# Seven-product weight units: two PSUM banks for the weight sums in place of three

## The reference, cut to what matters

```python
def swiglu(h, w_in, w_out):                      # first block, D_FF = 2816
    a, b = jnp.split(h @ w_in, 2, axis=-1)
    return (jax.nn.silu(a) * b) @ w_out
...
f = jnp.square(jax.nn.relu(h @ mlp_w1[i])) @ mlp_w2[i]     # second block, i = 0, 1; D_FF_2 = 4096
```

## Time and profile before

| what | value |
| --- | --- |
| median of 3 runs | 2633.7 us (2633.25 to 2634.71) |
| the profiled execution's own time | 2629.4 us |
| its span, first to last instruction | 2627.6 us |
| PE busy | 2569.7 us, 98% of the span |
| DVE, ACT, POOL busy | 53%, 45%, 41% |
| mean granted PE clock | 0.997 of full speed |
| HBM traffic | 102 GB/s over the span |

### The profile page before, as it was taken

The page is one execution under the profiler, slowest core; times in us unless marked ns, Lnnn a source line. Parts: engine busy times, 40 slices in busy tenths (PEclk is TensorE's granted clock), DMA queues, the critical chain, the costliest instruction groups (busy, mean ns, idle before and its releaser), DMA issues.

```text
span 2627.6 us, 40349 instructions
## 1 busy us (share of the span) xinstructions
PE 2569.7 (98%) x15940; PEld 2160.0 (82%) x15940; DVE 1388.7 (53%) x2479; ACT 1192.8 (45%) x2071; POOL 1076.0 (41%) x501
## 2 busy tenths in 40 slices
PE   8999999999999999999999999999999999999998
PEld 6887788888777777899977678899887778889997
DVE  4566543343533338353658857455445564744554
ACT  4454422222543345453543845445445774534543
POOL 2222343443323324464633634555542112555552
PEclk9999999999999999999999999999999999999999
DMA  8622244543222211232232022323331112232332
GB/s 325 239 97 96 96 161 151 198 160 114 92 73 73 73 65 58 83 118 94 96 100 96 18 73 93 100 87 99 112 105 61 45 49 73 87 103 86 104 103 82
DMA packets 49843, 271.62 MB, mean 103 GB/s; under 512 B 5583, under 2 KB 9319, under 8 KB 25608
## 3 DMA queue, kind: packets, MB, share of 16 engines
q1 hardware_dynamic: 45648, 265.71, 29.4%
q10 hardware_dynamic: 4024, 3.54, 0.6%
HBM read 267.09 MB, written 2.13 MB: 102 GB/s over the span
## 4 chain that ended last, share of the span: by engine, by line
PE 68%; issue 22%; POOL 5%; DVE 3%; ACT 1%; POOLq 0%; ACTq 0%; DVEq 0%
PE lin L879 14%; PE lin L881 13%; PE lin L880 13%; PE lin L1959 6%; PE lin L1960 6%; PE lin L1961 6%; POOL wlo L756 5%; PE lin L1431 2%; PE bank L1415 1%; PE bank L1449 1%; PE bank L1610 1%; PE bank L1028 0%; PE lin L1435 0%; PE bank L1602 0%; PE lin L1602 0%
## 5 line engine op out<-in xcount | busy, mean ns | idle before, releaser
L756 POOL TENSOR_TENSOR wlo<-raw,whi 128x1024 fp32r<-128x1024 f32 (+4 forms) x202 | 696.9, 3450 | 1309.7 <-ACT whi L2101 1309.7
L2101 ACT ACTIVATE whi<-raw 128x1024 fp32r<-128x1024 f32 (+4 forms) x202 | 295.4, 1462 | 601.1 <-PE lin L881 541.6
L879 PE MATMUL lin<-hhi,whi 128*128 128x512 f32 x1160 | 465.4, 401 | 7.4 <-issue 2.6
L881 PE MATMUL lin<-hhi,wlo 128*128 128x512 f32 x1160 | 453.3, 391 | 0.0
L880 PE MATMUL lin<-hlo,whi 128*128 128x512 f32 x1160 | 452.4, 390 | 0.0
L879 PE MATMUL lin<-ghi,whi 128*128 128x512 f32 x1136 | 445.8, 392 | 2.5 <-ACT m L2121 1.7
L881 PE MATMUL lin<-ghi,wlo 128*128 128x512 f32 x1136 | 442.3, 389 | 0.0
L880 PE MATMUL lin<-glo,whi 128*128 128x512 f32 x1136 | 442.2, 389 | 0.0
L777 POOL TENSOR_TENSOR wlo<-raw,whi 128x512 fp32r<-128x512 f32 x200 | 265.9, 1343 | 174.4 <-ACT whi L2433 172.2
L879 PEld LDWEIGHTS lin<-hhi,whi 128*128 128x128 f32 x1160 | 218.2, 188 | 68.6 <-issue 14.9
L881 PEld LDWEIGHTS lin<-hhi,wlo 128*128 128x128 f32 x1160 | 218.0, 188 | 47.1
(11 more groups left out here) (538 smaller groups left out, 4400.6 us busy)
## 6 DMA issues: line engine op xcount, KB each, us to landing
raw<-in_w SPq DMA_DIRECT2D x139, 1024.0 KB, 4.9
raw<-in_w SPq DMA_DIRECT2D x85, 512.0 KB, 3.6
adw_a<-in_ada SPq DMA_DIRECT2D x30, 1024.0 KB, 5.0
adw_b<-in_ada SPq DMA_DIRECT2D x18, 1024.0 KB, 5.5
raw<-in_w SPq DMA_DIRECT2D x12, 768.0 KB, 5.6
raw<-in_w SPq DMA_DIRECT2D x8, 640.0 KB, 3.9
raw<-in_w SPq DMA_DIRECT2D x8, 384.0 KB, 3.1
x<-in_x SPq DMA_DIRECT2D x1, 2048.0 KB, 9.8
```

The lines of the kernel that those rows point to most:

```text
L756: nc.gpsimd.tensor_tensor(wlo[:, slot, 0:size], raw[:, slot, 0:size], whi[:, slot, 0:size].bitcast(F32), ALU.subtract).then_inc(s.wlo_ok, 1)
L879: pe.matmul(dst, lh, rh, start=first, stop=False)
L881: return pe.matmul(dst, ll, rh, start=False, stop=last)
L2101: act.activation(whi[:, slot, 0:size], raw[:, slot, 0:size], ACT.Copy).then_inc(s.whi_ok, 1)
```

## The change

The third sum no longer has bank B7. It goes into B4, which sum 1 and low 1 used before it, and so can be made only after low 1 has read B4. The instruction moves from `seven_sums` into `block_low`, behind low 1, with a wait for sum 2 and for low 1. High 5 and low 5 read B4 in place of B7. In ACT's `mlp`, which prepares the first unit of the first run, high 2 and high 3 move from behind the sixth gate tile to behind the eighth. The waits in `block_high` stay as they are: high 2 still waits for the third sum.

```diff
@@ block_high (ACT)
-                       4: weight_block(u, 0, 1), 5: as_block(B7), 6: weight_block(u, 1, 1)}[k]
+                       4: weight_block(u, 0, 1), 5: as_block(B4), 6: weight_block(u, 1, 1)}[k]
@@ mlp (ACT)
-                    for j in {5: (0, 1, 2, 3), 7: (4, 5, 6)}.get(k, ()):
+                    for j in {5: (0, 1), 7: (2, 3, 4, 5, 6)}.get(k, ()):
                         block_high(st.u + 2, j)
@@ seven_sums (DVE)
                 v.tensor_tensor(as_block(B5), as_block(B4), weight_block(u, 0, 0), ALU.subtract).then_inc(s.sum_ok, 1)
-                v.wait_ge(s.sum_ok, HAD["sum_ok"] + 3 * g + 2)
-                v.tensor_tensor(as_block(B7), weight_block(u, 1, 0), as_block(B5), ALU.subtract).then_inc(s.sum_ok, 1)
@@ block_low (DVE)
-                v.tensor_tensor(block_of_four(wlo, b), as_block({1: B4, 2: B5, 5: B7}[k]), block_of_four(whi, b).bitcast(F32),
+                v.tensor_tensor(block_of_four(wlo, b), as_block({1: B4, 2: B5, 5: B4}[k]), block_of_four(whi, b).bitcast(F32),
                                 ALU.subtract).then_inc(s.blk_lo_v, 1)
+                if k == 1:
+                    v.wait_ge(s.sum_ok, HAD["sum_ok"] + 3 * g + 2)
+                    v.wait_ge(s.blk_lo_v, HAD["blk_lo_v"] + 3 * g + 1)
+                    v.tensor_tensor(as_block(B4), weight_block(u, 1, 0), as_block(B5), ALU.subtract).then_inc(s.sum_ok, 1)
```

## The result

The changed kernel takes **2679.89 us** (median of 4 runs, 2679.0 to 2681.97) against 2633.47 us (4 runs, 2632.56 to 2634.71): a ratio of 1.0181 [1.0169 to 1.0194], 46.4 us slower. The forecast was 2679 us. The profiled execution's span grew from 2627.6 to 2677.8 us; the granted clock is 0.997 of full speed in both.

What follows compares the result with a forecast made beforehand. PE, busy 98% of the span, was taken to bound the kernel. Terms 22.6 + 13.9 + 0.3 + 3.0 + 2.6 + 3 = 45.4, say 45 us, on a median of 2633.7 gave 2679 us, range 2662 to 2696.

Steps and rivals of the forecast that it cites:

- The chain: Third sum between low 1 and low 2 adds a second trip DVE, ACT, DVE; c22 comes 1.41 us later.
- Units inside a run: 1.16 us in each of 12 `ffn_short` units, 13.9 us; 1.41 us in each of 16 `mlp` units, 22.6 us.
- The slack of 0.32 us: In `ffn_short`, c22 would allow product 6 0.32 us before PE gets there; in `mlp` the slack is nil.
- the closed cycle: In `mlp`, product 6, results' work, sums, low 1, low 2, c22, product 6 form a loop, so each unit pays 1.41 us.
- The very first unit: First of the 50 units, where PE already waits on low 1, low 2 and c22: 3 us taken, upper bound 4.3.
- the upper bound's third term: In the very first unit, 1.44 us for twelve matmuls at half the clock, added to two chains of 1.41 us.
- First units of later runs: Product 6 comes late by 0.1 us in `ffn_short`, 0.43 in `mlp`; with stalls 0.3 us and 3.0 us in all.
- starts of `mlp`: First run of each `mlp`: two more high parts on ACT delay product 2 by 0.8 us; 1.3 us each, 2.6 together.
- signs named: PE waits for c22 about 40 us in some 36 places of 0.1 to 1.5 us; ACT waits for third sum 50 times.
- The clock did not fall at the stalls: Rival, 7%: PE's granted clock falls at each unit's stall, 52 us more in 36 units, 2731 us in all.
- Sum 1 did not get shorter by itself: Rival, 6%: on DVE sum 1 starts ahead of POOL's subtraction and takes about 0.70 us, not 1.80; time 2648 us.
- Low 1 did not move up: Rival, 5%: not slower, as low 1 on DVE starts 0.69 us earlier once sum 3 leaves; time stays at 2634 us.

Runs made afterwards that it cites:

- ACT's order alone: The kernel before with only ACT's order at the start of the first `mlp` run as in the change: 2633.79 us, 1.0006.
- the third experiment: The kernel before, three banks and third sum in its old place, but high 2 waits for low 1, ACT's `mlp` order as in the change: 2650.31 us, 1.0068.
- the best version: Changed kernel with third sum behind c22, POOL waiting for sum 1, DVE reordered in the very first unit and at `mlp` starts: 2627.56 us, 0.9982 against the kernel before.

## Why the prediction was right

**The chain** was right in kind, and a little short. Predicted: 1.41 us. Measured: the third sum starts 0.11 us after low 1 ends (1180.67 to 1180.78), not 0.04; all other steps are as predicted (0.70, then 0.09 from the sum's end at 1181.48 to high 2, 0.60, and 0.03 to low 2). C22 is 1.48 us later. The gap was taken from sums 1 and 2, where one semaphore is waited for; the third sum waits for two. The kernel before had rows nearer to the case: the second unit's sum 1, which waits for two semaphores, one of them given by low 5, starts 0.11 us after low 5 ends:

```profile
1051.23 0.68 DVE L3488 TENSOR_TENSOR wlo<-bank,whi 128x512 fp32r<-128x512 f32 x1
1052.02 0.70 DVE L3478 TENSOR_TENSOR bank<-raw 128x512 f32<-128x512 f32 x1
```

With this gap the predicted delay would have come out at 1.48 us. That the second semaphore is the reason was not tried.

**Units inside a run.** The slack of 0.32 us in `ffn_short` and of nil in `mlp` held, and so did the closed cycle: 11.31 and 11.64 us against 11.24 and 11.57 predicted, each 0.07 us more for the one gap. The terms become 12 x 1.23 = 14.8 us for 13.9, and 16 x 1.48 = 23.7 us for 22.6.

**The very first unit** was sized too small: its run grew by 6.3 us, and without two units of 1.23 us that leaves 3.8 us for it, inside the bounds of 1.4 and 4.3, but not the 3 taken. Its waits on PE, in the place of the earlier trace rows:

```profile
1045.40 0.39 PE L1959 MATMUL lin<-thi,whi 128*128 128x256 f32 x1 [1.30 <-DVE wlo L3486]
...
1051.35 0.44 PE L1959 MATMUL lin<-thi,whi 128*128 128x256 f32 x1 [4.26 <-DVE wlo L3486]
...
1061.39 0.36 PE L1959 MATMUL lin<-thi,whi 128*128 128x256 f32 x1 [2.53 <-DVE lin L3546]
```

The wait for low 2 went from 1.74 to 4.26 us, and that for c22 hardly changed, 2.42 and now 2.53 us. As predicted, high 2 holds up an activation on ACT (line 2249), and DVE stands idle for it ahead of low 2:

```profile
1047.88 0.69 DVE L3593 TENSOR_TENSOR sq<-tmp,lin 128x512 f32<-128x512 f32 x1 [1.73 <-ACT tmp L2249]
```

From product 0, low 2 came 2.4 us later by this, not one chain of 1.41 us, and c22 another 1.5 us later. Both delays together are the 3.9 us by which product 6 came later (18.9 us behind product 0, before 15.0), so the upper bound's third term, twelve matmuls at half the clock, did not come on top. The clock did fall behind both waits, where before it fell behind one, but behind low 2 PE's slower work fitted into the wait for c22. The third row is a stretch of the steady units:

```profile
1051.50:1055.00 3.50, 3.50 (x18) 3.50 (x19) 3.50 (x2) 0.37 (x1) 2.55 (x2) 0.51 0.59 180
1061.80:1065.30 3.50, 3.50 (x19) 3.50 (x18) 1.30 (x3) 1.31 (x3) 2.35 (x3) 0.52 0.00 0
1175.00:1185.00 10.00, 8.99 (x75) 8.82 (x74) 5.99 (x9) 5.52 (x12) 5.32 (x5) 1.00 0.32 107
```

The size of this term rests on one execution of each kernel. In the kernel with ACT's order alone, whose first run of units has the same instructions as before the change, the clock fell behind the wait for low 2 and not behind that for c22, and the run took 36.6 us instead of 38.2. Held against that one, it grew by 7.9 us.

**First units of later runs and starts of `mlp`.** The gaps of 0.1 and 0.43 us came out as 0.18 and 0.51, again by 0.07 or 0.08 for the one gap. The starts gave 0.84 us from product 1 to product 2 where 0.8 was predicted, and ACT's order alone gave 0.74. As a whole the two starts gave 1.8 and 1.5 us beside their two units of 1.48, where 1.3 was predicted; where the difference of 0.3 us between them comes from stays open. Two of the later `mlp` runs grew by only 3.0 us: 0.5 us that product 2 lost there, behind other work of DVE (line 4023), is gone.

**The sum** of what the runs grew by is 48.4 us, the predicted terms 45.4. The medians differ by 46.4 us and the spans by 50.2; the profiled execution of before was among the shortest (2629.4 us by its own time against a median of 2633.47). That 2679 was met to a microsecond is luck: it hides some 3 us of terms too small. Of the signs named, the waits for c22 came as said (39.8 us in 37 places, the longest 2.5 us in the very first unit, against 1.5 named), and ACT waited for the third sum 47 times instead of 50.

**The rivals.** The clock did not fall at the stalls of the steady units: it is at 1.00 in the stretch 1175 to 1185 us, with a stall of 1.01 us in it. Among the seven-product units it falls only in the very first, behind the waits of 4.26 and 2.53 us. The Trainium skill, "TensorE: Matmul & The Clock Gate", Part 1, calls the throttled clock the default that activity has to lift. The rows agree behind these two waits; stalls of 1.0 to 1.34 us in each unit did not bring that default back. The prediction's rows for the short waits were one execution: in the kernel with ACT's order alone the clock stood at 0.50 behind the wait of 1.74 us, which it had passed at 1.00 in the kernel before:

```profile
1052.60:1056.00 3.40, 3.40 (x17) 3.40 (x18) 3.40 (x2) 0.37 (x1) 2.51 (x2) 0.50 0.54 176
```

Sum 1 did not get shorter by itself (1419 ns in the mean, 1414 before): POOL's subtraction still starts 0.05 us ahead of it, since both hang on ACT, and an edit was needed to part them. Low 1 did not move up: it stands 0.72 us of idle time behind sum 2, held by high 1, as the rows of before said. The Trainium skill, "VectorE: DVE Perf Modes", "The DRAIN you can't avoid", by which a semaphore behind each instruction costs nothing, holds within DVE to 0.04 us behind sum 1 and 0.11 us behind low 1, and a row that has nothing left to wait for starts even 0.08 us before the one ahead of it ends (c22 at 1182.81, behind low 2), so a wait within DVE is cheap here but not free. The page does not speak of a hand-off to another engine and back, which the third experiment prices at 0.71 us.

## What to carry to other kernels

Where the engine that bounds the kernel shows almost no waits, the slack of the chain that feeds it still has to be read from a timeline: here it was 0.32 us and nil, so 1.48 us of new latency became 1.23 and 1.48 us in each unit, though no instruction had been added. When a buffer is given up, place the late producer behind the consumer that the bounding engine waits for, and move the wait with it to the instruction that needs it: the same sharing then cost nothing. An instruction that fills an idle gap for free (0.72 us, while DVE waits for high 1) gives nothing back when it leaves, so at its new place it costs its whole length.

## What the runs showed of the hardware that was not expected

- An addition of two blocks in SBUF takes 0.69 us on DVE alone and 1.80 us when a subtraction on POOL starts 0.04 or 0.05 us ahead of it; a subtraction with one operand in a bank takes 0.70 us either way (sum 2 and the third sum). That one wait on POOL would return 28 us was not foreseen.
- Dependent instructions on DVE follow each other after 0.04 us (sum 1, sum 2) and after 0.11 us (low 1, third sum; low 5, sum 1).
- The granted clock held at 1.00 through a stall of 1.0 us in each unit of 11.3 us, and was 0.51 and 0.52 behind waits of 4.26 and 2.53 us. In the best version, three waits of 0.53 to 1.15 us at the same place left it at 1.00; with ACT's order alone it was 0.50 behind a wait of 1.74 us, across which it stayed at 1.00 in the kernel before.
